# One written order for each engine instead of one for all: mixer and expert jobs of a diffusion step on one core

## The reference, cut to what matters

```python
def layer(x, mod, P, rope, k_ext, v_ext):
    h = rmsnorm(x, P['norm_mix_g']) * (1.0 + sc_m) + sh_m
    proj = h @ P['w_in']
    # attention (8 query heads on 2 key heads, latents also see 128 cached keys),
    # a long convolution by cosine/sine matrices, chunked gMLP
    ...
    mixed = jnp.concatenate([attn, hy, sg], axis=-1) @ P['w_out']
    x = x + g_m * mixed
    h = rmsnorm(x, P['norm_ffn_g']) * (1.0 + sc_f) + sh_f
    x = x + g_f * peer(h, P['peer_wq'], P['peer_keys'], P['peer_u'], P['peer_v'])

def peer(h, wq, keys, u_tab, v_tab):
    # per token and head: two top-16 of 128 scores, top-16 of their 256 sums -> 16 experts
    a = gelu(einsum('td,ted->te', xt, u_tab[it]))     # 8 heads x 16 experts
    return einsum('te,ted->td', gate * a, v_tab[it])
```

## Time and profile before

| | us |
|---|---|
| median of 3 runs | 4169.28 |
| lowest, highest | 4165.45, 4172.28 |
| the profiled execution's own time | 4163.25 |
| its span in the trace | 4161.4 |

### The profile page before, as it was taken

One profiled execution on the slowest core, in us unless ns is written; L12 is line 12 of the kernel. 1 busy time (PEld: TensorE's weight loads), 2 busy tenths in 40 slices (PEclk: granted clock), 3 DMA queues, 4 the chain that ended last, 5 costly groups with the idle time before them and its releaser, 6 DMA issues.

```text
span 4161.4 us, 33677 instructions
## 1 busy us (share of the span) xinstructions
PE 3145.0 (76%) x9680; PEld 1439.0 (35%) x9680; DVE 2890.9 (69%) x6522; ACT 1039.7 (25%) x2232; POOL 2554.8 (61%) x2564
## 2 busy tenths in 40 slices
PE   6796686477778787777778977866777777777777
PEld 4653543233333333222233435432222222222223
DVE  2388889555667567888763689887667666767672
ACT  4322422212222222222222325211222222222222
POOL 0055566345666566766676556757777777777774
PEclk9898997689999999999999989978999999999999
DMA  7687788999999999999999788979999999999998
GB/s 283 225 315 287 249 298 308 355 381 363 387 351 389 369 403 399 401 381 354 363 392 370 264 321 309 340 274 379 408 406 399 409 406 399 409 408 397 410 408 309
DMA packets 394007, 1485.63 MB, mean 357 GB/s; under 512 B 44125, under 2 KB 46879, under 8 KB 377953
## 3 DMA queue, kind: packets, MB, share of 16 engines
q0 software_dynamic: 368640, 1342.34, 84.0%
q1 hardware_dynamic: 25184, 141.13, 8.7%
HBM read 1480.42 MB, written 2.88 MB: 356 GB/s over the span
## 4 chain that ended last, share of the span: by engine, by line
DMA 30%; PE 19%; POOL 17%; DVE 16%; issue 12%; ACT 4%; SPq 0%; DVEq 0%; ACTq 0%; POOLq 0%
DMA rows_ring<-in_peer_v,idx 19%; POOL rows_ring L680 17%; PE psum L984 10%; DMA rows_ring<-in_peer_u,idx 8%; DVE rows_ring L1560 5%; DVE mix L1574 3%; PE psum L770 3%; DMA rows_ring<-in_peer_v,idx_c 1%; PE psum L757 1%; DMA rows_ring<-in_peer_u,idx_c 1%; DVE small L1475 1%; ACT area L1189 1%; DMA ring<-in_ada 1%; PE psum L726 1%; PE psum L719 1%
## 5 line engine op out<-in xcount | busy, mean ns | idle before, releaser
L984 PE MATMUL psum<-rows_ring,diag 128*128 128x512 f32 x4096 | 2046.7, 630 | 690.1 <-DMA rows_ring<-in_peer_v,idx 507.6
L1560 DVE SCALAR_TENSOR_TENSOR rows_ring<-rows_ring,psum 128x1024 f32<-128x1024 f32 x1024 | 1245.1, 1220 | 651.5 <-DMA rows_ring<-in_peer_u,idx 612.7
L984 PEld LDWEIGHTS psum<-rows_ring,diag 128*128 128x128 f32 x4096 | 726.9, 194 | 1944.9 <-DMA rows_ring<-in_peer_v,idx 1159.3
L680 POOL DMA_INDIRECT rows_ring<-in_peer_u,idx x1024 | 976.9, 954 | 478.4 <-issue 271.5
L680 POOL DMA_INDIRECT rows_ring<-in_peer_v,idx x1024 | 968.9, 946 | 485.8 <-PE psum L984 277.6
L1225 ACT ACTIVATE diag<-ident,wts 128x128 f32<-128x128 f32 x1024 | 380.4, 397 | 1297.9 <-PE psum L984 1297.2
L680 POOL DMA_INDIRECT rows_ring<-in_peer_u,idx_c x256 | 322.3, 1259 | 433.7 <-DVE idx_c L1547 202.6
L770 PE MATMUL psum<-area,ring 128*128 128x128 f32 (+1 forms) x1344 | 385.6, 446 | 20.6 <-ACT area L1075 18.8
L680 POOL DMA_INDIRECT rows_ring<-in_peer_v,idx_c x256 | 286.6, 1119 | 185.1 <-DVE mix L1574 128.8
L1574 DVE SCALAR_TENSOR_TENSOR mix<-rows_ring,wts,mix 128x1024 f32<-128x1024 f32 x254 | 326.3, 1285 | 21.2 <-DMA rows_ring<-in_peer_v,idx_c 19.0
L1560 DVE SCALAR_TENSOR_TENSOR rows_ring<-rows_ring,area 128x1024 f32<-128x1024 f32 x256 | 312.3, 1223 | 22.9 <-DMA rows_ring<-in_peer_u,idx_c 21.2
(11 more groups left out here) (201 smaller groups left out, 2407.4 us busy)
## 6 DMA issues: line engine op xcount, KB each, us to landing
ring<-in_ada SPq DMA_DIRECT2D x48, 1024.0 KB, 9.0
ring<-in_win SPq DMA_DIRECT2D x32, 1024.0 KB, 8.2
ring<-in_wout SPq DMA_DIRECT2D x16, 1024.0 KB, 8.2
ring<-in_wq SPq DMA_DIRECT2D x16, 1024.0 KB, 7.8
rows_ring<-in_peer_u,idx POOLq DMA_INDIRECT x1024, 7.4
rows_ring<-in_peer_v,idx POOLq DMA_INDIRECT x1024, 7.4
ring<-in_dft SPq DMA_DIRECT2D x12, 1024.0 KB, 8.2
rows_ring<-in_peer_u,idx_c POOLq DMA_INDIRECT x256, 6.3
```

Of the source, the lines that this page charges most:

```text
L680: pool.indirect_dma_start(row(table, k), None, (peer_u, peer_v)[table], bass.IndirectOffsetOnAxis(ap=idx_of(grp, u)[:, k:k + 1], axis=0)). ...
L984: m = pe.matmul(acc[:, b, :], diag[:, k % 4, :], row(1, k)[:, b * 512:(b + 1) * 512], start=(u % PEER_HEADS == 0 and k == 0), stop=last)
L1560: dve.scalar_tensor_tensor(out=row(0, k), in0=row(0, k), scalar=1.0, in1=h, op0=ALU.mult, op1=ALU.mult, accum_out=dots[:, k:k + 1]).then_i ...
```

## The change

- `weave`, `ROOM` and the single `ORDER` go. There are two lists, `MIXERS` and `EXPERTS`, and for each of PE, ACT and DVE a table of counts (`TURNS_PE`, ...): so many jobs of the mixer list, then so many of the expert list, and so on. Within either list the order is the same on all engines; how the two mesh is not. Banks are read from a string of digits (`BANKS`).
- The expert steps are one list over all 80 units. Step 8 has the dots of unit 8 and the adds of unit 7, and so at 40 and 48. POOL's loop runs on in the same way: before the v rows of unit s-1 it waits for the row numbers of unit s, also over a group's end.
- Within a step, DVE's weights of unit s-1 come behind the first dot of unit s (`dots` has two buffers now), the gelu at the end of the step.
- The norm is in pieces: `rms` in four jobs of two chunks, `rsd` for the rstd, `xm` for DVE's products, `xn` for scale and shift. Its work is the same.
- The bank wait in front of `kb` is left out where there is no earlier user; three waits are added (`h_ready` before `ht`, `v_free` before the first add of a group on PE and on DVE).

No arithmetic, load or matmul is added or removed. Where the tables put the mixers, counted out against the expert list ("41.8" is behind dot 8 of step 41):

| | PE | DVE |
|---|---|---|
| latents, layer 0: first filter job | before step 0 | 0, ahead of seven of the eight pick parts of unit 0 |
| its attention | before step 0 | 2.7 to 3.12 |
| its second norm, last score copy | 8.0 (first job of the step) | 5.1, 6.4 |
| context, layer 1: norm to last scores | 9.5 to 14.1 | 9.12 to 14.2 |
| latents, layer 1: filter | 30.7 to 31.3 | 30.8 to 30.13 |
| its norm and projections | 41.2 | 41.8 to 44.4 |
| its attention | 41.2 | 44.4 to 45.13 |
| its second norm, then its first score copy | 48.0 | 47.5, 47.15 |

PE has no part in context steps, so "before step 0", "8.0", "41.2" and "48.0" mean that it does these jobs as they become ready. ACT has the mixer jobs of these stages in blocks at the beginning of each context step.

```diff
-def weave(mixer, experts):
...
-ORDER = mixer_jobs(0, C_)
...
+def step_jobs(s):
+
+    cur, prev, nxt = (ALL_UNITS[i] if 0 <= i < len(ALL_UNITS) else None for i in (s, s - 1, s + 1))
+    jobs, ahead, own = [], None, None
+    if cur:
+        grp, u = cur
+        latent = GROUPS[grp][1] == L_
+        if u == 0 and grp not in PICKED_AHEAD:
+            jobs += pick_jobs(grp, 0)
+        if latent and u % PEER_HEADS == 0:
+            jobs += [("ht", grp, u // PEER_HEADS, half) for half in range(2)]
+        if grp + 1 in PICKED_AHEAD and 0 <= u - AHEAD_FROM < UNITS[grp + 1]:
+            ahead = (grp + 1, u - AHEAD_FROM)
+        own = nxt if nxt and nxt[0] == grp and grp not in PICKED_AHEAD else None
     for p in range(PIECES):
...
+        jobs += [("dot", *cur, p)] if cur else []
+        if p == 0:
+            jobs += [("weigh", *prev, 0)] if prev else []
+            jobs += [("gexp", *cur, 0)] if cur and cur[0] not in PICKED_AHEAD else []
+        jobs += [("add", *prev, p)] if prev else []
+        if p == 2 and s > 1 and ALL_UNITS[s - 2][1] % PEER_HEADS == PEER_HEADS - 1:
+            grp, u = ALL_UNITS[s - 2]
+            jobs += [("bk", grp, u // PEER_HEADS, half) for half in range(2)]
...
+    jobs += [("gelu", *cur, 0)] if cur else []
...
+MIXERS = []
 for _l in range(DEPTH):
...
+    MIXERS += mixer_jobs(_l, C_) + (filter_jobs(_l) if _l else []) + mixer_jobs(_l, L_)
+EXPERTS = [job for s in range(len(ALL_UNITS) + 1) for job in step_jobs(s)]
...
+TURNS_PE = (
+    251, 337, 42, 64, 1, 2, 2, 3, 11, 11, 4, 4, 2, 4, 3, 8, 3, 5, 2, 6, 2, 5, 4, 5, 2, 3, 2, 3, 3, 4, 1, 2, 1, 2, 3, 8, 3, 3, 2, 2, 3, 6,
...
+def in_turns(turns):
+
+    out, at = [], [0, 0]
+    for i, n in enumerate(turns):
+        out += (MIXERS, EXPERTS)[i % 2][at[i % 2]:at[i % 2] + n]
+        at[i % 2] += n
+    return out
+
+
+ORDER = {"PE": in_turns(TURNS_PE), "ACT": in_turns(TURNS_ACT), "DVE": in_turns(TURNS_DVE)}
...
-            for grp in range(len(GROUPS)):
-                for u in range(UNITS[grp] + 1):
-                    if u < UNITS[grp]:
-                        pool.wait_ge(s["idx_ready"], PICK[grp, u] + 1)
-                    for k in range(TOPK):
-                        if u < UNITS[grp]:
-                            fetch(0, grp, u, k)
-                        if u > 0:
-                            fetch(1, grp, u - 1, k)
+            for i in range(len(ALL_UNITS) + 1):
+                if i < len(ALL_UNITS):
+                    pool.wait_ge(s["idx_ready"], PICK[ALL_UNITS[i]] + 1)
+                for k in range(TOPK):
+                    if i < len(ALL_UNITS):
+                        fetch(0, *ALL_UNITS[i], k)
+                    if i > 0:
+                        fetch(1, *ALL_UNITS[i - 1], k)
...
+                pe.wait_ge(s["h_ready"], KC * done("rsd", l, L_, 1))
...
-            for job in ORDER:
+            for job in ORDER["PE"]:
```

199 lines of the change are left out of this document (81 added, 118 removed), and 15 rows, old and new, of tables (TURNS_ACT, TURNS_DVE, TURNS_PE).

## The result

The changed kernel takes 4194.6 us (median of 7 runs, 4188.0 to 4206.6); the kernel before, run beside it, 4170.4 us (7 runs, 4165.5 to 4177.9). The ratio is 1.0056, with a 95% interval of 1.0043 to 1.0069: the change makes the kernel 0.6% slower. The forecast was 4100 us, in a range of 4010 to 4180.

The account below looks back on a forecast made before the run. Row transfers were taken as the bound, 405 GB/s when clean. Terms -12, -22, +19, -46 and -3 sum to -64 us: 4099 profiled, 4105 for the median, 5 more off gives 4100 us, range 4010 to 4180.

Parts of the forecast that it names:

- Clean stretch, weights one dot later: Latent units with no mixer beside them: weights come 1.3 us later on DVE, PE takes it back, cost 0.
- Latents' mixer of layer 0: Units 0 to 7: last scores out at 649, dots of unit 8 end at 793 against 805, 12 us gained.
- No PE mixer hides or delays that: After the last scores of layer 0: DVE's remaining 138 us of work up to unit 8's dots runs unhindered by PE.
- Units 9 to 39: From 805 to 2261, bound by transfers, context mixer of layer 1 squeezed into steps 9.5 to 14.1: 22 us gained.
- a rate of 405 in steps 15 to 25: Sign that the forecast is right: transfers run at 405 GB/s from step 15 to 25.
- Joint at unit 40: Adds of unit 39 beside dots of unit 40: tile back after 54 us, so layer 1's mixer starts 19 us later.
- Mixer of layer 1: Latents' mixer beside units 40 to 47: 46 us less, between 15 and 75; row numbers about 439 us after the tile's return.
- 3 us of gain: Joint at unit 48: its dots and unit 47's adds in one step, 41.4 us and 5, against 46 for dots alone.
- The port: POOL's gather issue, 954 ns beside latent and 1259 beside context units: the trace shows 305 ns, not a whole 1.2 us.
- The rival: Gather issue becomes the bound beside context units, each waiting a whole DVE instruction, 2.17 us: 4400 us, chance 0.02.
- Slower: Squeezed mixer, steps 9.5 to 14.1 on PE ahead of the adds, costs more than the rest gives: 4200 us, chance 0.08.
- the orders differ but wait alike: Attention stays at 136 and 122 us, set by ACT's chain, and the window loses 70: 4180 us, chance 0.09.

Follow-up runs that it names:

- early weights: Changed kernel with DVE's weights and ACT's exp of the next unit's gates back at the end of the unit's own step: 4090.3 us, again 4093.4 us.
- one order: Changed kernel with weights early and one common job order for PE, ACT and DVE: 4170.4 us; with the context mixer of layer 1 ending at unit 14, 4172.8 us.

## Why the prediction was wrong

It had the sign wrong by one term. The rest of the sum came out near (-64 forecast, -72 with early weights without the last row), but partly by luck: the first row was 18 us too hopeful and the second 35 us too cautious. By the ends of dots (profiled executions; "early" is the change with early weights):

| | predicted | after | early |
|---|---|---|---|
| to the dots of unit 8 (795) | -12 | +6 | +6 |
| dots of 8 to dots of 39 (1466) | -22 | -16 | -57 |
| to the dots of unit 48 (566) | -30 | -16 | -21 |
| clean stretch and end (1334) | 0 | +69 | +2 |
| sum | -64 | +43 | -70 |

- *Clean stretch, weights one dot later: the term that failed.* It was put at 0 because an add takes 1.78 us of the 2.6 that it has the earlier trace rows, and PE so takes 1.3 us back. Three things were missed. The dot in front doesn't cost its own 1.3 us but 2.6, one period of the rows, since it waits 1.33 us for its row (2.3 in the net, as the wait for the gelu falls away). The exp of the gates with its table load hangs behind the weights, so the lateness adds to 2.8 us of path that were there already and uses up the rest of the slack. And PE, after a stand of 3 us, mostly comes back at the lower clock level, at which an add takes 3.7 us, so that it takes nothing back. The cost was 2.1 us (1.7 in the kernel before) in each of 31 clean units and 42 us more in units 8 to 39. The argument on slack was the right kind: at 0.7 us more (with the exp moved away) it holds to the us in the clean stretch. It needed the whole path, not the instruction that was moved. The trace of before shows the table load behind the weights, and the prediction never said what stands between the weights and the first diagonal.
- *Latents' mixer of layer 0.* The chain went as forecast or better, the time didn't: -12 forecast, +6 measured. Of these 18 us 10 are the mark: 793 was set against 805, and against the true 795.3 only 2 us were to be gained. The rows are PE's first attention scores, wo, and the last scores:

```profile
379.18 3.88 PE L880 MATMUL psum<-area 64*128 64x128 f32 x16 [1.87 <-DVE mix L1430]
...
487.22 55.20 PE L759 MATMUL psum<-mix,ring 128*128 128x512 f32 x128 [0.79 <-DVE mix L1486]
...
632.07 2.06 PE L953 MATMUL psum<-ring,mix 64*128 64x128 f32 x32 [0.33 <-issue]
```

  Attention took 108 us where I had put 105 (136 before), wo began at 487 ("near 500"), and the last scores were out at 634 instead of 649. But the dots of unit 8 then took 167 us more, where 143 were forecast. The work left to DVE at 634 was just what the prediction had counted, 43 dots and 43 adds. The step that failed is "No PE mixer hides or delays that": DVE stands 21.4 us for one product of the next mixer (the context's, layer 1: its modulation rows), whose turn on DVE comes ahead of those dots, and PE in turn waits 15.6 us for the first weights of that product:

```profile
649.68 1.94 PE L715 MATMUL psum<-ring,cwide 128*32 128x512 f32 x8 [15.55 <-DMA ring<-in_ada]
```
```profile
DVE modT L1295 <- PE psum L722: 21.4, 1, 21.4
```

  With early weights this wait is 19.6 us, and in the kernels with one order, whose first stretch is 22 us shorter, it doesn't occur. Moving these few jobs behind the dots of unit 8 is the next thing to try. While the chain was quicker, the units beside it got less: 217 GB/s in the attention, against 252 before.

```profile
379.18:487.22 108.04, 81.72 (x768) 69.25 (x768) 91.13 (x182) 60.77 (x134) 49.99 (x41) 0.98 0.65 217
```

- *Units 9 to 39.* -22 was too small once late weights are taken out: -57. The turns did free units 15 to 24 (405 GB/s at full clock, as forecast), and the filter's stretch gained 11 us for 7. In the changed kernel itself the late weights took 41 of the 57 back. I had written that a rate of 405 in steps 15 to 25 would show me right; it was 383 (1193 to 1587), so that sign pointed at the fault.
- *Joint at unit 40.* The tile was back 52 us behind the dots of unit 39, forecast 54. Right.
- *Mixer of layer 1.* From the tile's return to the row numbers of unit 48: 444 us, forecast 439, with 111 us for the attention (forecast 105). Right in its parts. The dots of unit 48 then took 54 us instead of 46, where 3 us of gain were forecast: the adds of unit 47 now stand between them on DVE (busy 46.1 of 47 us), while PE does nothing from 2757 to 2804 (last but one row of the first table).
- *The port.* A gather's issue beside context units takes 1240 ns (u rows; v rows 1159), against 1259 before and 952 beside latent units. The prediction took the difference of the means, some 0.3 us, for the price of one meeting. But the mean hides two kinds of issue. Of 512 issues beside context units, 134 began at least 0.1 us behind the start of a dot or add with both inputs in SBUF that had 0.3 us or more to go: every one of them took the rest of that instruction and 0.81 us. The others mostly took 0.94. The group, one of the 134, and the DVE instruction that it met (until 2324.44):

```profile
L670 POOL DMA_INDIRECT rows_ring<-in_peer_u,idx_c x256 | 317.4, 1240 | 444.6 <-DVE idx_c L1546 211.3
```
```profile
2323.52 1.74 POOL L670 DMA_INDIRECT rows_ring<-in_peer_u,idx_c  x1 [1.19 <-DVE rows_ring L1559]
```
```profile
2323.17 1.27 DVE L1574 SCALAR_TENSOR_TENSOR mix<-rows_ring,wts,mix 128x1024 f32<-128x1024 f32 x1
```

  The Trainium skill, "SBUF — State Buffer", section "SBUF: two separate sides", has a DVE instruction with two SBUF inputs and a POOL instruction that reads SBUF exclude each other, whichever starts first, for the whole instruction. The trace agrees for POOL's issues that come second. It doesn't show DVE held up: its dots take 1222 ns beside context units and 1219 beside latent ones. The rival still falls, as it needed a whole instruction at every issue, and the means hardly moved with the change (v rows took 1119 before).

- *The rivals.* None describes what happened. "Slower" was looked for in the squeezed mixer, which cost nothing with turns (385 us in units 8 to 15, 383 before), and "the orders differ but wait alike" is refuted by the attention, which took 108 and 111 us instead of 136 and 122 or more, and by the 464 us of the one order in the place where the turns took 385. No rival stood against the term of 0, which is why the range missed too.

What stays open: how the 77 to 81 us split between the turns as such, their placement by hand in other stretches than units 8 to 24, and the banks dealt with them; and norm in pieces, which no kernel took out.

## What to carry over

Before a step is moved by "one small instruction", follow everything that is chained behind it to the point where a buffer comes free: here a dot, a table load, an exp and a diagonal. Slack in a ring has an end: in clean units 0.7 us too late cost nothing and 2.3 us cost 2.1 us in every unit, more than half of it through the clock. The remedy was to take a table load off the path or to leave the step in its place. Where one change has many parts, a term of nought that is repeated 64 times deserves its own rival. Engines that each have their own order pay off where one would otherwise stand for another's product with transfers to serve behind it; a single job placed too early in such an order cost 20 us here. And a mean over two kinds of case is the price of neither.

## What the runs showed of the hardware

PE's granted clock fell behind a stand of 3.06 us (0.56 and 0.58 in the 8 us from 3332 on at unit 60, 1.00 ahead of them). It did so at 23 of 29 unit boundaries of the changed kernel, and at 19 of 29 of the kernel before with late weights, whose stands are as long; in 28 of 29 steps with stands of some 1.4 us (exp moved) it stayed at 1.00. The price comes behind the gap and not in it: five matmuls in 4.61 us against eight in 3.68. With the gap filled by idle matmuls it stayed at 1.00, and that was worth 1.35 us of the 2.1 a unit, though PE did more work. A gather's issue on POOL that met a running DVE instruction with both inputs in SBUF took the rest of it and 0.81 us, 134 times of 134. A table load on ACT took 1.28 us, and the exp behind it began at once (3331.20 and 3332.50 at unit 60).
